# Residual tiles split between VectorE and ScalarE, and a recurrence moved behind the next turn's first convolution

## What is computed

```
block 1:  u = rms(h) @ w_in; Hyena (FFT filters) and bidirectional mLSTM from u
          h = h + mixed @ w_out
          h = h + cross_attention(rms(h), rms(mem))
          h = h + square(relu(rms(h) @ ff_w1)) @ ff_w2
          x = rms(h, final_norm_g)
block 2:  u = rms(x, ln1_g) @ w_in_2, cut in seven parts b_a, c_a, x_a, x_b, g_b, ga, gb
          A = c_a * conv3(b_a * x_a)
          v = conv4(x_b) + bias; r = sigmoid(Wa v), i = sigmoid(Wx v), block-diagonal
          a = exp(-8 r softplus(-lam)); s_t = a_t s_(t-1) + sqrt(1 - a_t^2) (i v)_t
          B = s * gelu(g_b)
          x = x + (sigmoid(ga) (A @ woa) + sigmoid(gb) (B @ wob)) @ w_o_2
          x = x + (silu(n @ w_gate) * (n @ w_up)) @ w_down, n = rms(x, ln2_g)
          out = rms(x, final_g_2)
```

## Time and profile before

| what | us |
|---|---|
| median of three runs | 1944.73 |
| profiled execution | 1949.02 |
| its span, first to last instruction | 1947.2 |
| TensorE busy (91% of the span) | 1776.1 |
| VectorE busy (54%) | 1055.6 |
| ScalarE busy (30%) | 584.5 |
| GpSimd busy (39%) | 753.2 |

### The profile page before, as it was taken

One profiled execution on the slowest core, in us unless ns is written; L12 is line 12 of the kernel. 1 busy time (PEld: TensorE's weight loads), 2 busy tenths in 40 slices (PEclk: granted clock), 3 DMA queues, 4 the chain that ended last, 5 costly groups with the idle time before them and its releaser, 6 DMA issues.

```text
span 1947.2 us, 21967 instructions
## 1 busy us (share of the span) xinstructions
PE 1776.1 (91%) x7718; PEld 1433.0 (74%) x7718; DVE 1055.6 (54%) x1379; ACT 584.5 (30%) x709; POOL 753.2 (39%) x312
## 2 busy tenths in 40 slices
PE   6799988975889998999999789898999999999996
PEld 4677876654667677888888577676888888888885
DVE  5751487879782566233248867575533463133137
ACT  2322332332212221111111254646433233122221
POOL 3432441113333143444444244444544444444442
PEclk9899998987899998999999899999999999999998
DMA  4232220110222022222222122223222222222222
GB/s 156 87 109 76 96 78 33 44 44 32 87 97 76 33 92 71 97 97 97 97 97 97 65 87 93 102 86 104 91 97 97 97 95 96 94 95 96 97 97 97
DMA packets 47694, 169.28 MB, mean 87 GB/s; under 512 B 5204, under 2 KB 5204, under 8 KB 47320
## 3 DMA queue, kind: packets, MB, share of 16 engines
q1 hardware_dynamic: 44640, 160.45, 23.6%
q10 hardware_dynamic: 3000, 8.09, 1.2%
HBM read 166.43 MB, written 2.10 MB: 87 GB/s over the span
## 4 chain that ended last, share of the span: by engine, by line
issue 31%; PE 29%; POOL 13%; DVE 1%; POOLq 0%; ACT 0%; DVEq 0%
POOL m_w_lo L433 13%; PE ps L465 10%; PE ps L467 10%; PE ps L466 10%; DVE m_h L1917 0%; DVE m_s L1187 0%; POOLq L441 0%; POOLq L439 0%; POOL m_QL L453 0%; DVE m_qs L1559 0%; PE ps L493 0%; DVE m_qs L1561 0%; DVE m_s L1894 0%; DVE m_ftmp L1551 0%; DVE m_ftmp L1549 0%
## 5 line engine op out<-in xcount | busy, mean ns | idle before, releaser
L433 POOL TENSOR_TENSOR m_w_lo<-m_raw,m_w_hi 128x1024 fp32r<-128x1024 f32 x302 | 738.8, 2450 | 1119.1 <-ACT m_w_hi L875 1119.1
L875 ACT ACTIVATE m_w_hi<-m_raw 128x1024 fp32r<-128x1024 f32 x302 | 317.7, 1056 | 761.4 <-DMA m_raw<-in_strips 757.6
L465 PE MATMUL ps<-m_XH,m_w_hi 128*128 128x512 f32 x1160 | 474.4, 409 | 36.6 <-POOL m_w_lo L433 22.5
L466 PE MATMUL ps<-m_XL,m_w_hi 128*128 128x512 f32 x1160 | 458.8, 396 | 0.0
L467 PE MATMUL ps<-m_XH,m_w_lo 128*128 128x512 f32 x1160 | 458.6, 395 | 0.0
L465 PEld LDWEIGHTS ps<-m_XH,m_w_hi 128*128 128x128 f32 x1160 | 222.7, 192 | 101.0 <-POOL m_w_lo L433 27.2
L466 PEld LDWEIGHTS ps<-m_XL,m_w_hi 128*128 128x128 f32 x1160 | 223.0, 192 | 47.6 <-issue 2.7
L467 PEld LDWEIGHTS ps<-m_XH,m_w_lo 128*128 128x128 f32 x1160 | 222.0, 191 | 47.9
L465 PE MATMUL ps<-m_FH,m_w_hi 128*128 128x512 f32 x432 | 168.9, 391 | 3.3 <-DVE m_FL L1180 3.2
L466 PE MATMUL ps<-m_FL,m_w_hi 128*128 128x512 f32 x432 | 168.6, 390 | 0.0
L467 PE MATMUL ps<-m_FH,m_w_lo 128*128 128x512 f32 x432 | 168.5, 390 | 0.0
(11 more groups left out here) (311 smaller groups left out, 2295.8 us busy)
## 6 DMA issues: line engine op xcount, KB each, us to landing
m_raw<-in_strips SPq DMA_DIRECT2D x302, 512.0 KB, 3.2
m_x_in<-in_x ACTq DMA_DIRECT2D x8, 256.0 KB, 4.6
m_x_res<-in_x ACTq DMA_DIRECT2D x1, 2048.0 KB, 8.0
out<-m_h SPq DMA_DIRECT2D x8, 256.0 KB, 2.1
m_memf<-in_mem ACTq DMA_DIRECT2D x1, 1024.0 KB, 10.4
m_decay<-in_decay ACTq DMA_DIRECT2D x1, 1024.0 KB, 15.1
m_w<-in_w ACTq DMA_DIRECT2D x1, 512.0 KB, 13.6
m_skip<-in_skip ACTq DMA_DIRECT2D x1, 512.0 KB, 3.9
```

The source lines that it names most:

```text
L433: nc.gpsimd.tensor_tensor(w_lo[:, c], raw[:, c], f(w_hi[:, c]), ALU.subtract).then_inc(lo_ready, 1)
L465: pe.matmul(dst, w_hi[:, c], xh, start=first, stop=False)
L466: pe.matmul(dst, w_hi[:, c], xl, start=False, stop=False)
L875: act.activation(w_hi[:, c], raw[:, c], ACT.Copy).then_inc(hi_ready, 1)
```

## The change

In the residuals and at the join ScalarE now makes the high half (a copy with the gain as scale) and the squares; VectorE keeps the add, the low half and the sums. ScalarE's part is `tiles_out`, which also takes the conversions that stood there before. At the join the second square, with the gain `fin_g` as its scale, goes to `e1`. The last FFN chunk does the same without the split. VectorE's loops over two groups of four tiles are written out. The sums start with a copy in place of a cleared buffer. In the recurrent stage gelu goes from in front of the sigmoids to behind the root, the sixth conversion (`ahead(n + 5)`) goes from behind the square to behind the sigmoids, and VectorE's recurrence of turn mt-1 stands between the three taps of turn mt and its second bank.

```diff
+            def tiles_out(r, s, e, gain, dh, first=0, second=None):
+
+                for u in range(KT):
+                    if u >= first and s + u + 3 < N_STRIPS:
+                        ahead(s + u)
+                    act.wait_ge(evac, e + u + 1)
+                    if dh is not None:
+                        act.activation(tile(dh, u), tile(h, u), ACT.Copy, scale=gain(u)).then_inc(x_high, 1)
+                    if u >= 2:
+                        act.wait_ge(summed, 8 * r + u - 1)
+                    act.activation((s0, s1)[u % 2][:], tile(h, u), ACT.Square).then_inc(squared, 1)
+                    if second is not None:
+                        if u:
+                            act.wait_ge(summed_two, u)
+                        act.activation(e1[:], tile(h, u), ACT.Square, scale=second(u)).then_inc(squared_two, 1)
...
-            for u in range(1, N_SQ):
-                ahead(S_WOUT + u)
+            tiles_out(0, S_WOUT, E_WOUT, lambda k: col("x_g", k), YH, first=1)
...
-            squares(S_XO, N_SQ // 4)
+            tiles_out(1, S_XO, E_XO, lambda k: col("ff_g", k), YH)
...
-            squares(S_FF, N_FF // 4)
+            squares(S_FF, N_FF // 4 - 2)
+            act.wait_ge(gain_two, 1)
+            tiles_out(2, S_FF + 56, E_FF + 56, lambda k: misc[:, k:k + 1], XH, second=lambda k: col("fin_g", k))
...
-                act.wait_ge(in_free[4], mt + 1)
-                act.activation(t2[5][:], t2[4][:], ACT.Gelu_apprx_tanh).then_inc(gelu_out, 1)
                 act.wait_ge(pe_done, n + 6)
                 act.activation(t2[6][:], ps[:, 5, :], ACT.Sigmoid, bias=col("ba", mt)).then_inc(achain, 1)
                 act.activation(t2[7][:], ps[:, 6, :], ACT.Sigmoid, bias=col("bx", mt)).then_inc(gates_free, 1)
+                ahead(n + 5)
                 act.wait_ge(gates_free, mt + 1)
                 act.activation(t2[8][:], t2[6][:], ACT.Exp, scale=misc[:, 56 + mt:57 + mt]).then_inc(lru_a, 1)
                 act.activation(t2[10][:], t2[6][:], ACT.Tanh, scale=misc[:, 48 + mt:49 + mt]).then_inc(achain, 1)
                 act.wait_ge(lru_a, mt + 1)
                 act.activation(a_sq[:], t2[8][:], ACT.Square).then_inc(lru_e, 1)
-                ahead(n + 5)
                 act.wait_ge(lru_q, mt + 1)
                 act.activation(l_root[:], s0[:], ACT.Sqrt).then_inc(lru_r, 1)
+                act.wait_ge(in_free[4], mt + 1)
+                act.activation(t2[5][:], t2[4][:], ACT.Gelu_apprx_tanh).then_inc(gelu_out, 1)
...
-            squares(S_WO2, N_SQ // 4)
+            tiles_out(3, S_WO2, E_WO2, lambda k: col("ln2_g", k), XH)
...
-                    for u in range(8):
-                        ahead(s + u)
+                    tiles_out(4, s, e - 8, None, None)
...
-            def residual(first_s, first_e, gain, dh, dl, src=h):
-
-                ch.sync()
-                ch.add(dve.memset(acc[:], 0.0))
-                with ch.loop(2, 12) as i:
-                    for u in range(4):
-                        hm = h[:, bass.ds(i * (4 * T) + u * T, T)]
-                        dve.wait_ge(pe_done, i * 4 + (first_s + u + 1))
-                        dve.tensor_tensor(hm, src[:, bass.ds(i * (4 * T) + u * T, T)], ps[:, u, :], ALU.add
-                                          ).then_inc(evac, 1)
-                        dve.wait_ge(evac, i * 4 + (first_e + u + 1))
-                        ch.sync()
-                        split(dh[:, bass.ds(i * (4 * T) + u * T, T)], dl[:, bass.ds(i * (4 * T) + u * T, T)], hm,
-                              dcol(gain, i * 4 + u), x_ready)
-                        add_squares(hm)
-                ch.sync()
+            def add_square(r, u):
+
+                dve.wait_ge(squared, 8 * r + u + 1)
+                x = (s0, s1)[u % 2]
+                if u:
+                    dve.wait_ge(summed, 8 * r + u)
+                    dve.tensor_tensor(acc[:], acc[:], x[:], ALU.add).then_inc(summed, 1)
+                else:
+                    dve.tensor_copy(acc[:], x[:]).then_inc(summed, 1)
+
+            def residual(r, first_s, first_e, gain, dh, dl, src=h):
+
+                ch.sync()
+                for u in range(KT):
+                    dve.wait_ge(pe_done, first_s + u + 1)
+                    dve.tensor_tensor(tile(h, u), tile(src, u), ps[:, u % 4, :], ALU.add).then_inc(evac, 1)
+                    dve.wait_ge(evac, first_e + u + 1)
+                    dve.wait_ge(x_high, 8 * r + u + 1)
+                    dve.scalar_tensor_tensor(tile(dl, u), tile(h, u), gain(u), f(tile(dh, u)), ALU.mult, ALU.subtract
+                                             ).then_inc(x_ready, 1)
+                    add_square(r, u)
+                dve.wait_ge(summed, 8 * r + KT)
                 dve.sem_inc(norm_sum, 1)
 
             dve.wait_ge(ld_h, 16)
-            residual(S_WOUT, E_WOUT, "x_g", YH, YL, x_res)
+            residual(0, S_WOUT, E_WOUT, lambda k: col("x_g", k), YH, YL, x_res)
...
-            ch.add(dve.memset(acc[:], 0.0))
-            ch.add(dve.memset(e0[:], 0.0))
-            with ch.loop(2, 6 * 4) as i:
-                for u in range(4):
-                    to = bass.ds(i * (4 * T) + u * T, T)
-                    hm = h[:, to]
-                    n = 48 + 8 + u
-                    dve.wait_ge(pe_done, i * 4 + (S_FF + n + 1))
-                    dve.tensor_tensor(hm, hm, ps[:, u, :], ALU.add).then_inc(evac, 1)
-                    dve.wait_ge(evac, i * 4 + (E_FF + n + 1))
-                    ch.sync()
-                    ch.add(dve.tensor_scalar(s0[:], hm, dcol("fin_g", i * 4 + u), None, ALU.mult))
-                    split(XH[:, to], XL[:, to], hm, misc[:, bass.ds(i * 4 + u, 1)], x_ready)
-                    add_squares(hm)
-                    ch.sync()
-                    add_squares(s0[:], e0)
-            ch.sync()
+            for u in range(KT):
+                n = 48 + 8 + u
+                dve.wait_ge(pe_done, S_FF + n + 1)
+                dve.tensor_tensor(tile(h, u), tile(h, u), ps[:, u % 4, :], ALU.add).then_inc(evac, 1)
+                dve.wait_ge(evac, E_FF + n + 1)
+                dve.wait_ge(x_high, 16 + u + 1)
+                dve.scalar_tensor_tensor(tile(XL, u), tile(h, u), misc[:, u:u + 1], f(tile(XH, u)),
+                                         ALU.mult, ALU.subtract).then_inc(x_ready, 1)
+                add_square(2, u)
+                dve.wait_ge(squared_two, u + 1)
+                if u:
+                    dve.wait_ge(summed_two, u)
+                    dve.tensor_tensor(e0[:], e0[:], e1[:], ALU.add).then_inc(summed_two, 1)
+                else:
+                    dve.tensor_copy(e0[:], e1[:]).then_inc(summed_two, 1)
+            dve.wait_ge(summed, 16 + KT)
+            dve.wait_ge(summed_two, KT)
...
+            def recurrence(mt):
+
+                dve.wait_ge(lru_r, mt + 1)
+                ch.add(dve.tensor_tensor(t2[7][:], t2[7][:], l_root[:], ALU.mult))
+                ch.sync()
+                ch.add(dve.tensor_tensor_scan(s0[:], t2[8][:], t2[7][:], 0.0, ALU.mult, ALU.add))
+                ch.sync()
+                dve.wait_ge(gelu_out, mt + 1)
+                ch.add(dve.tensor_tensor(t2[7][:], s0[:], t2[5][:], ALU.mult))
+                ch.sync()
+                split(tile(BH, mt), tile(BL, mt), t2[7][:], 1.0, b_ready)
...
                 conv_step(t2[1], pX[:, 0:T], "cb0", t2[0]).then_inc(u_full, 1)
+                if mt:
+                    recurrence(mt - 1)
                 dve.wait_ge(pe_done, n + 2)
...
-                dve.wait_ge(lru_r, mt + 1)
-                ch.add(dve.tensor_tensor(t2[7][:], t2[7][:], l_root[:], ALU.mult))
-                ch.sync()
-                ch.add(dve.tensor_tensor_scan(s0[:], t2[8][:], t2[7][:], 0.0, ALU.mult, ALU.add))
-                ch.sync()
-                dve.wait_ge(gelu_out, mt + 1)
-                ch.add(dve.tensor_tensor(t2[7][:], s0[:], t2[5][:], ALU.mult))
-                ch.sync()
-                split(tile(BH, mt), tile(BL, mt), t2[7][:], 1.0, b_ready)
-                dve.wait_ge(a_ready, mt + 1)
-                dve.wait_ge(b_ready, mt + 1)
+            recurrence(KT - 1)
+            dve.wait_ge(a_ready, KT)
+            dve.wait_ge(b_ready, KT)
...
+                if not last:
+                    with dve.Fori(0, 2) as i:
+                        for u in range(4):
+                            hm = h[:, bass.ds(i * (4 * T) + u * T, T)]
+                            dve.wait_ge(pe_done, i * 4 + (s + u + 1))
+                            dve.tensor_tensor(hm, hm, ps[:, u, :], ALU.add).then_inc(evac, 1)
+                else:
+                    for u in range(KT):
+                        dve.wait_ge(pe_done, s + u + 1)
+                        dve.tensor_tensor(tile(h, u), tile(h, u), ps[:, u % 4, :], ALU.add).then_inc(evac, 1)
+                        if u:
+                            add_square(4, u - 1)
+                    add_square(4, KT - 1)
```

(19 more changed lines are left out.)

## The result

The changed kernel takes 1909.44 us (median of 4 runs, 1909.1 to 1914.87), the kernel before beside it 1944.67 us (4 runs, 1944.56 to 1947.07): ratio 0.9822, 95% interval 0.9803 to 0.9842. The profiled execution took 1909.1 us, its span is 1907.3 us at a mean granted clock of 0.963.

What follows compares the result with a forecast made beforehand. TensorE was taken to set the end, stalled by waits, with the recurrent stage bound by a serial ScalarE-VectorE chain. Gains of 9.5 + 17.9 + 8.0 = 35.4 us off 1944.7 gave 1909.3 us, range 1896 to 1923.

Steps and rivals of the forecast that it cites:

- Join, 17.9 us: Join of the two blocks: TensorE's stall goes, so `pX`, and the recurrent stage with it, comes 17.9 us earlier.
- First residual, 9.5 us, handover at nothing: First residual: strip 1's regular matmul comes 9.5 us earlier; ScalarE's delayed third conversion costed at nothing, up to 3 us.
- The residuals behind cross-attention and before the FFN, and the end, 0: Residuals without a TensorE wait gain nothing; the end's chain stays one of three: 0, between -0.3 and +0.3 us.
- The turn, 32.5: Recurrent stage: one turn, the spacing of `pX`, falls from 33.45 to 32.5 us.
- the walk: Recurrent stage: operation-by-operation timing of ScalarE, VectorE and GpSimd through one turn, with four lock holds, together 7.2 us.
- Seven turns give 7 x 0.95 = 6.7: Recurrent stage: seven turns each 0.95 us shorter give 6.7 us; with the earlier `BH` strip, 8.0 taken.
- TensorE waits 3.9 us in each turn: Before the gate's strip in each turn TensorE waits 3.9 us and may fall to 1.2 GHz, +2.8 us a strip.
- From profile to median: Whole kernel: the median of the runs lies 4.3 us under the profiled execution, so 1944.7 - 35.4 = 1909.3 us.
- (a): Rival, recurrent stage: the turn does not shorten, only residuals and tail gain, 1916 us; chance 0.20.
- (b): Rival, recurrent stage: locks fall well, the turn is TensorE's 28.6 to 29 us, 1884 us in all; chance 0.07.
- (c): Rival, residuals: handover too slow, last tiles stay late and half the stalls stay, 1923 us; chance 0.07.
- (d): Rival, recurrent stage: all six subtractions hold an operation for their full 2.3 us, turn 39 us, 1957 us; chance 0.03.

Runs made afterwards that it cites:

- the run with short subtractions: Kernel before, with GpSimd subtracting 128 of 1024 columns for strips of the first block's FFN and the first two turns: 1907.24 us (one run).

## Why the prediction was right

The forecast was 1909.3 us and the time is 1909.44, and most steps hold. Two of the agreements are luck, errors that cancel: the split of the turn's gain and the step from profile to median.

- **Join, 17.9 us.** 17.7. Both parts are as said: ones-matmul 5.44 behind strip 0, strip 1 at full clock. Of the two causes named for the old stall, the locks made most of it (the run with short subtractions), the eight operations 1.9 us at most. For the first residual no run took the two apart.
- **First residual, 9.5 us, handover at nothing.** 9.5 for the boundary, but strip 0 starts 0.9 us later after `w_out`'s start than it did: 8.6 net. I had allowed up to 3 if the cover went. VectorE caught up later than "by the sixth tile": its last `YL` was held (1.58 us) and the last sum ended at 567.96, 1.1 us before the ones-matmul.
- **The residuals behind cross-attention and before the FFN, and the end, 0.** From the first residual to the join 0.0. At the end TensorE's wait for the last sum is 2.24 us, before 2.48; the other 0.3 of the last row lie elsewhere behind `BH`.
- **The turn, 32.5.** 32.47, with exactly the four holds of the walk: 2.23 for the first convolution step, 3.56 for the next two, 2.73 for the product with gelu, 2.12 for `yA`. The scan stands free at 1.23.
- **"Seven turns give 7 x 0.95 = 6.7", the whole 8.0.** The whole is 8.2, the split is wrong. There are six intervals of 32.47 (6 x 0.98 = 5.9 won), a first one 9.8 shorter, and a last stretch 7.4 longer. The walk from which I took 259.0 had this (259.33 measured), the sentence had not: for two turns or for twenty it would have misled.
- **TensorE waits 3.9 us in each turn.** They are 3.5 in three turns and 2.0 in four. The low clock does follow, in four of the seven: seven or eight matmuls start 0.43 us apart and the strip takes 7.1 to 7.2 us instead of 5.6, so 1.6 us where I had 2.8. The slack covers it, as said, and at the strip for `BH` a wait of 1.06 us stays, where I had up to 1.8.
- **From profile to median.** I carried over the 4.3 us by which the profiled execution of before lay above its median. That of after lies 0.3 below its own. The span therefore fell by 39.9 instead of 35.4. The untouched front of the kernel gave 4.8 of this, and the parts that I had summed came to 35.1.

Of the rivals, (a), a turn that keeps 33.45, is what the kernel with the residuals alone shows, and the changed kernel doesn't. (b), TensorE's bound in the turn, can be reached, but by another order. (c) and (d) had no trace: no half stall, and four holds on the chain where (d) wanted six.

What I missed is that **the two edits of the turn work against each other**. The prediction weighed them as one and never asked for each alone. "The recurrence is moved along the chain, not off it" stands there as a point for (a); followed through for ScalarE's order alone it gives 30.8 us a turn, which I worked out only ahead of that run (31.09 measured).

The lock is the mechanism behind most of this. The Trainium skill (SBUF — State Buffer, SBUF: two separate sides) says that an operation of VectorE with two inputs in SBUF and a GpSimd operation that reads SBUF shut each other out for a whole instruction. The rows agree. In the changed kernel the product at L1869, which reads PSUM, took 0.68 us at 1179.29, inside a subtraction that began at 1178.82, and `yA` behind it, on SBUF alone, took 2.12 (rows of POOL, then of DVE):
```profile
1171.11 2.39 POOL L439 TENSOR_TENSOR m_w_lo<-m_raw,m_w_hi 128x1024 fp32r<-128x1024 f32 x1 [3.03 <-ACT m_w_hi L881]
1178.82 2.75 POOL L439 TENSOR_TENSOR m_w_lo<-m_raw,m_w_hi 128x1024 fp32r<-128x1024 f32 x1 [5.32 <-ACT m_w_hi L881]
...
1178.62 0.75 DVE L1843 SCALAR_TENSOR_TENSOR m_t<-m_pA,m_const,m_s 128x512 f32<-128x512 f32 x1
1179.29 0.68 DVE L1869 TENSOR_TENSOR m_e<-ps,m_rstd 128x512 f32<-128x512 f32 x1
1180.01 2.12 DVE L1872 TENSOR_TENSOR m_yA<-m_e,m_t 128x512 f32<-128x512 f32 x1
```

Open: how the 3.9 us of the changed turn divide between the held operations and the late `w_lo`. No run took away one hold at a time. Open too: why the front of the kernel, which no edit touches, was 4.8 us shorter in one trace than in the other.

## What to carry to other kernels

Before moving a block of work, write down what the other engine does beside it in the old place and in the new one; a block that stays on the chain gains only what it covers, and here ScalarE's reordering without the move was worth twice what both gave in the stage. Try each of two joint edits alone. Where two engines share a lock, don't count holds but ask which held operation somebody waits for, and place the others under the lock.

## What the runs showed of the hardware

- The lock works in both directions. The product with gelu at 1171.32 came 0.2 us behind the start of GpSimd's subtraction (1171.11, 2.39 us) and ended 0.55 us after it. Where VectorE was first (its step at 1178.62 ran to 1179.37), GpSimd's subtraction took 2.75 us (1178.82) instead of 2.40.
- The price of a hold doesn't depend on the size of what is held. An operation of 8 columns that takes 0.17 us alone took 2.35 (719.18, kernel before), a 128x512 product of 0.69 us took 2.73.
- Code that is the same takes a different time in different traces, early in the kernel. The ones-matmul of the first residual, with the same code up to it, stands at 569.04 us in the changed kernel and at 569.85, 570.53, 571.29, 572.34 and 573.28 in five of the others, a spread of 4.2 us. The runs of one kernel spread over 8 (the kernel before, 1944.22 to 1952.27), so the program need not be the reason. The cause stays open; later stages are best compared from a mark inside each trace.
